# A hybrid layer's expert stage: rows spread over the dense blocks, half of the late query products moved into the second stage

## The reference, cut to what matters

```python
q = einsum('td,de->te', xb, w_q).reshape(T, 8, 2, 128)        # 8 heads, 2 halves
s = einsum('thpd,hpkd->thpk', q, keys)                         # 128 keys per half
s_top, i_top = top_k(s, 16)                                    # per half
best, sel = top_k(all 16 x 16 sums of the two halves, 16)
gate = softmax(best)
act = gelu(einsum('td,thkd->thk', xb, u_tab[eidx]))            # dot with the expert's row u
out = einsum('thk,thkd->td', gate * act, v_tab[eidx])          # weighted sum of the rows v
```

## Time and profile before

| what | value |
|---|---|
| median of 3 runs | 2141.62 us (2140.74 to 2150.80) |
| profiled execution, its own time | 2143.07 us |
| its span in the profile | 2141.0 us |
| TensorE matmul busy | 1934.9 us, 90% of the span |
| VectorE busy | 1358.9 us, 63% |
| ScalarE busy | 616.4 us, 29% |
| GpSimd busy | 675.5 us, 32% |
| DMA | 629.25 MB, mean 294 GB/s |
| granted TensorE clock, mean | 0.972 of full speed |
| dense stage (144 blocks) | about 844 to 1531 us |
| second stage (384 rows) | about 1535 us to the end |

### The profile page before, as it was taken

The page is one execution under the profiler, slowest core; times in us unless marked ns, Lnnn a source line. Parts: engine busy times, 40 slices in busy tenths (PEclk is TensorE's granted clock), DMA queues, the critical chain, the costliest instruction groups (busy, mean ns, idle before and its releaser), DMA issues.

```text
span 2141.0 us, 29757 instructions
## 1 busy us (share of the span) xinstructions
PE 1934.9 (90%) x10912; PEld 1564.2 (73%) x10912; DVE 1358.9 (63%) x2860; ACT 616.4 (29%) x1217; POOL 675.5 (32%) x556
## 2 busy tenths in 40 slices
PE   5998889988996988999999999998899998999886
PEld 4997889978966988998999999998544433434332
DVE  3219263353345535488988888988377777776663
ACT  4223312252224324444445444445300000000000
POOL 0003012100000000232333233232277776776663
PEclk9999899988998999999999999999999999999999
DMA  3557158637614573899999999999499999999997
GB/s 117 197 198 220 31 180 260 216 86 257 237 41 178 177 261 119 318 366 349 403 388 361 388 394 357 376 364 376 184 412 403 404 407 412 397 398 415 405 414 290
DMA packets 244650, 629.25 MB, mean 294 GB/s; under 512 B 19714, under 2 KB 137541, under 8 KB 226712
## 3 DMA queue, kind: packets, MB, share of 16 engines
q0 software_dynamic: 74880, 377.52, 44.5%
q1 hardware_dynamic: 169632, 249.92, 34.4%
HBM read 584.36 MB, written 110.21 MB: 324 GB/s over the span
## 4 chain that ended last, share of the span: by engine, by line
DMA 19%; PE 15%; DVE 14%; issue 7%; ACT 2%; POOL 2%; SPq 1%; DVEq 1%; another core or an unknown queue 0%; ACTq 0%; POOLq 0%
DMA ex_w_raw<-in_peer_ut 10%; DMA ex_uv_row<-value_rows,ex_eidx 9%; PE ps L2137 9%; DVE ex_fin L2388 4%; DVE ex_w_lo L1935 3%; POOL ex_uv_row L2066 2%; PE ps L589 2%; PE ps L590 2%; PE ps L591 2%; DVE ex_uv_row L2376 2%; ACT ex_w_hi L2199 1%; DVE ex_q_s L2401 1%; DVE ex_top_i L2335 0%; SPq L1989 0%; DVEq L162 0%
## 5 line engine op out<-in xcount | busy, mean ns | idle before, releaser
L2137 PE MATMUL ps<-ex_uv_row,ex_q_s 128*128 128x512 f32 (+1 forms) x1208 | 542.4, 599 | 61.3 <-DVE ex_q_s L2401 47.3
L2137 PEld LDWEIGHTS ps<-ex_uv_row,ex_q_s 128*128 128x128 f32 (+1 forms) x1208 | 217.1, 187 | 366.3 <-issue 347.6
L2066 POOL DMA_INDIRECT ex_uv_row<-value_rows,ex_eidx x384 | 405.2, 1055 | 214.6 <-issue 102.2
L589 PE MATMUL ps<-x_hi,ex_w_lo 128*128 128x384 f32 (+2 forms) x1296 | 427.6, 330 | 27.8 <-DVE ex_w_lo L1935 22.6
L590 PE MATMUL ps<-x_lo,ex_w_hi 128*128 128x384 f32 (+2 forms) x1296 | 423.6, 327 | 0.0
L591 PE MATMUL ps<-x_hi,ex_w_hi 128*128 128x384 f32 (+2 forms) x1296 | 423.5, 327 | 0.0
L2050 POOL DMA_INDIRECT ex_uv_row<-in_peer_uv,ex_eidx x128 | 190.6, 1489 | 410.2 <-DVE ex_fin L2388 404.7
L2388 DVE SCALAR_TENSOR_TENSOR ex_fin<-ex_uv_row,ret_tables,ex_fin 128x1024 f32<-128x1024 f32 x218 | 278.7, 1279 | 0.3
L589 PEld LDWEIGHTS ps<-x_hi,ex_w_lo 128*128 128x128 f32 x1296 | 244.6, 189 | 40.7 <-DVE ex_w_lo L1935 30.7
L591 PEld LDWEIGHTS ps<-x_hi,ex_w_hi 128*128 128x128 f32 x1296 | 245.0, 189 | 0.0
L590 PEld LDWEIGHTS ps<-x_lo,ex_w_hi 128*128 128x128 f32 x1296 | 244.8, 189 | 0.0
(11 more groups left out here) (415 smaller groups left out, 3418.5 us busy)
## 6 DMA issues: line engine op xcount, KB each, us to landing
value_rows<-in_peer_uv SPq DMA_DIRECT2D x64, 1024.0 KB
ex_w_raw<-in_peer_ut SPq DMA_DIRECT2D x128, 512.0 KB
value_rows<-ex_z_rows SPq DMA_DIRECT2D x128, 128.0 KB
first_raw<-in_w_in SPq DMA_DIRECT2D x8, 1024.0 KB, 7.9
ex_w_raw<-in_peer_wq SPq DMA_DIRECT2D x16, 512.0 KB
value_rows<-ex_z_rows SPq DMA_DIRECT2D x128, 64.0 KB
dp_w_raw<-in_w_in SPq DMA_DIRECT2D x14, 512.0 KB
ex_uv_row<-value_rows,ex_eidx POOLq DMA_INDIRECT x384
```

The costliest lines, as they stand in the source:

```text
L589: pe.matmul(out, left(llo, c), right(rhi, c), start=(c == 0), stop=False)
L2066: pool.indirect_dma_start(value_slot(p)[0], None, k.value_rows, bass.IndirectOffsetOnAxis(ap=eidx[:, u, n % TOPK:n % TOPK + 1], axis=0), e ...
L2137: ins = pe.matmul(k.pv[j % 2][0:r, c, :], spread[:, on_tensor[p] % SPREADS, 0:r], v[:, c * 512:(c + 1) * 512], start=first, stop=last)
```

## The change

It has five parts. (1) The last four heads' query blocks ("first", 8 of them) compute in the dense stage only the 136 columns of tile 0 and the sample tile. The 384 columns of tiles 1 to 3 ("rest", 8 blocks) come in the second stage, one in front of rows 8, 17, ..., 71 of it, with their 512 KB of weights loaded, rounded and lowered again. (2) The columns of the tokens are laid out as tile 0, sample, tiles 1 to 3, so that the first four heads' query blocks too are now two groups, of 136 and 384 columns, in place of 260 and 260. (3) Rows begin at block 6, none stands at a block whose number is a multiple of 16, and so 130 rows stand beside the dense blocks; the last 6, all of the sample tile, come behind them. (4) VectorE makes a block's lower half ahead of that block's dot. (5) 9 more rows of the second stage go to VectorE, and `norm_final` is loaded into the buffer `x_rep`, once all 136 dots are made. Three of the eight rest blocks' weights are still loaded beside the dense blocks, and two of them lowered there; SyncE loads the other five behind the results of the first two tiles.

```diff
-ROWS_FROM = 8
+ROWS_FROM = 6
+FULL = 4
+QUERY_ROWS = [8 + 9 * n for n in range(2 * (PH - FULL))]
...
-    for u in range(PH - 1):
-        out += [("q", 2 * (u + 1) + j // 3) if j in (0, 3) else ("z", next(z)) for j in range(TOPK)]
-    return out + [("z", n) for n in z]
+    for u in range(1, PH):
+        kind = "q" if u < FULL else "first"
+        out += [(kind, 2 * u + j // 3) if j in (0, 3) else ("z", next(z)) for j in range(TOPK)]
+    return out + [("z", n) for n in z], [("rest", n) for n in range(2 * FULL, HP)]
...
+    row_at = dict(zip((i for i in range(ROWS_FROM, B) if i % TOPK), range(PAIRS)))
+    beside = len(row_at)
+    query_at = {PAIRS + m: B + n for n, m in enumerate(QUERY_ROWS)}
...
-    by_vector = {*range(HK), *(rests - late), *range(SLOTS - VECTOR_LAST, SLOTS)}
+    more = {PAIRS + m for m in range(12, QUERY_ROWS[-1] + 9) if m % TOPK in (5, 13)}
+    by_vector = {*range(HK), *(rests - late), *more, *range(SLOTS - VECTOR_LAST, SLOTS)}
...
-        x_rep, gain = sb("x_rep", [P, D])[:, :], w_raw[1][:, :, :].rearrange("p c n -> p (c n)")
+        x_rep, gain = [sb("x_rep", [P, D])[:, :]] * 2
...
-        tile = lambda t: slice(t * P, t * P + ROWS[t])
+        at_column = lambda t: t * P + (NS if 0 < t < TILES else 0) if t < TILES else P
+        tile = lambda t: slice(at_column(t), at_column(t) + ROWS[t])
...
-                    if i == len(blocks) - 1:
-                        lowered(sp, len(blocks) - 2)
-                        sp.dma_start(gain, a["norm_final"].unsqueeze(0).to_broadcast([P, D])).then_inc(gain_loaded, 16)
                 store(blocks[-1][1])
-                for j in range(NT):
+                sp.wait_ge(dotted, PAIRS)
+                sp.dma_start(gain, a["norm_final"].unsqueeze(0).to_broadcast([P, D])).then_inc(gain_loaded, 16)
+                result(0)
+                result(1)
+                for i in range(B + DEEP, len(all_blocks)):
+                    load(i)
+                for j in range(2, NT):
                     result(j)
...
-                def queries(i, n):
+                def queries(i, kind, n):
                     lowered(pe, i)
-                    for h in range(2):
-                        wait(pe, q_done, 2 * n + h - 1)
-                        mm3(pe, k.pb[4 + h][:, 0:HALF], DC, lambda x, c: x[:, c, :], w_hi[i % DEEP], w_lo[i % DEEP],
-                            lambda x, c: x[:, c, h * HALF:(h + 1) * HALF], x_hi, x_lo).then_inc(q_mm, 1)
+                    if kind != "rest":
+                        wait(pe, q_done, n)
+                        mm3(pe, k.pb[4][:, 0:P + NS], DC, lambda x, c: x[:, c, :], w_hi[i % DEEP], w_lo[i % DEEP],
+                            lambda x, c: x[:, c, 0:P + NS], x_hi, x_lo).then_inc(q_mm, 1)
+                    if kind != "first":
+                        wait(pe, rest_done, n)
+                        mm3(pe, k.pb[5][:, 0:BT], DC, lambda x, c: x[:, c, :], w_hi[i % DEEP], w_lo[i % DEEP],
+                            lambda x, c: x[:, c, P + NS:T], x_hi, x_lo).then_inc(rest_mm, 1)
...
                 for p in range(PAIRS, SLOTS):
                     u, i = divmod(order[p], TOPK)
+                    if p in query_at:
+                        queries(query_at[p], *all_blocks[query_at[p]])
                     if p not in by_vector:
                         add_row(p)
...
+                    if query_at.get(p + 6, 0) >= B + 2:
+                        upper(query_at[p + 6])
+                    if p - 2 in query_at:
+                        take(*all_blocks[query_at[p - 2]])
...
-                for i in range(len(blocks)):
-                    p = i - ROWS_FROM
-                    if 0 <= p < PAIRS:
+                for i in range(B):
+                    p = row_at.get(i, -1)
+                    if i + 2 >= 5:
+                        lower(dve, i + 2)
+                    if p >= 0:
                         dot(p)
-                    if 5 <= i + 2 < len(blocks) and by_dve(i + 2):
-                        lower(dve, i + 2)
                     if 0 < p <= HK:
                         add_vector(p - 1)
...
-                for p in range(len(blocks) - ROWS_FROM, PAIRS):
+                for p in range(beside, PAIRS):
                     dot(p)
...
                 for p in range(PAIRS, SLOTS):
                     u, i = divmod(order[p], TOPK)
+                    if query_at.get(p + 4, 0) >= B + 2:
+                        lower(dve, query_at[p + 4])
                     picked(p)
```

More of the change, by code:

```diff
@@ L1999, in _ @@
                 for i, (kind, n) in enumerate(blocks):
[L2000 to L2001 removed]
+                    load(i + DEEP)
                     if i and blocks[i - 1][0] == "z":
@@ L2173, in _ @@
                 for i, (kind, n) in enumerate(blocks):
-                    if kind == "q":
-                        queries(i, n)
+                    if kind == "z":
+                        activities(i, n)
                     else:
-                        activities(i, n)
+                        queries(i, kind, n)
                     if i in scores_at:
                         scores(scores_at[i])
-                    if HK <= i - ROWS_FROM - 1 < PAIRS:
-                        add_row(i - ROWS_FROM - 1)
-                for p in range(len(blocks) - ROWS_FROM - 1, PAIRS):
+                    if row_at.get(i, 0) > HK:
+                        add_row(row_at[i] - 1)
+                for p in range(max(HK, beside - 1), PAIRS):
                     add_row(p)
@@ L2283, in _ @@
                     elif i:
-                        take(blocks[i - 1][1], 0)
-                        take(blocks[i - 1][1], 1)
-                    if i and i + 2 < len(blocks):
+                        take(*blocks[i - 1])
+                    if i:
                         upper(i + 2)
-                    if 0 <= i - ROWS_FROM < PAIRS:
-                        row(i - ROWS_FROM)
+                    if i in row_at:
+                        row(row_at[i])
                     if i in weight_at:
@@ L2480, in _ @@
                         normalise(normalise_at[i])
-                for p in range(len(blocks) - ROWS_FROM, PAIRS):
+                for p in range(beside, PAIRS):
                     dot(p)
+                    if p <= HK:
+                        add_vector(p - 1)
+                    if p == HK:
+                        add(0)
                 scale(0)
```

43 lines of the change are left out of this document (23 added, 20 removed).

## The result

| | before | after |
|---|---|---|
| median of 4 runs (lowest to highest) | 2141.18 us (2125.25 to 2150.80) | 2212.48 us (2204.76 to 2227.20) |
| profiled execution, its span | 2143.07, 2141.0 us | 2204.76, 2202.7 us |

What follows compares the result with a forecast made beforehand. The prediction took TensorE to lead in the dense stage, DMA and VectorE close, and DMA behind row 80. From 2143.07 us, -24 and +23.2 gave 2142.3, forecast as 2141 us, no measurable change; range 2120 to 2162.

Steps and rivals of the forecast that it cites:

- Lower half ahead of the dot: VectorE's dense-stage order: loads come a dot (1.22 us) earlier behind retrieval pieces, at most 4.9 us per period; nothing more counted.
- the weight loads decide: Rival, chance 0.26: weight loads landing near 13 us keep the four dense periods near 73 us; total about 2155 us.
- dense stage: Sum of the terms up to the last dense block: -24 us, with ends -6 and -40.
- passage: From the last dense block to the first value row: late `norm_final` delays `scale(0)`; +9.5 us, ends 4 and 17.
- first 80 rows: Start of the second stage: eight rest blocks add 33.8 us to TensorE, nine moved rows take 16.1 off; +17.7 us.
- behind row 80: Rest of the second stage: DMA bounds again, with ten rows ahead instead of seven or eight; -4 us, ends 0 and -10.
- second stage: Sum of everything behind the dense stage, passage included: +23.2 us, ends +12 and +32.
- 136 columns at 0.112 us: Query blocks' small matmuls: assumed to start every 0.112 us, as for 128 columns, making a first block 2.7 us.
- TensorE's 71.1 become 65.0: Blocks 50 to 114: TensorE's need per 16 blocks falls thus, period 74.25 to 69.5 us, gaining 19 us in all.
- TensorE leads: Dense stage before: TensorE's need per 16 blocks, 71.1 us, is the largest, ahead of DMA's 68.7 and VectorE's 64.6.
- The rest blocks are free: Rival, chance 0.11: ten slots and TensorE's idle time absorb them; second stage costs 10 instead of 23.2; total 2128 us.
- the dense stage reaches the DMA floor: Rival, chance 0.18: the four periods fall to 67 us, the last stretch gives all 10.9, passage 5 cheaper; total 2123 us.

Runs made afterwards that it cites:

- e2: The kernel before with only VectorE's lower half moved ahead of the dot: 2207.62 us, ratio 1.0307 to the kernel before.
- e5: The changed kernel, lower half still first, with ScalarE making at each block the coefficient of the row before: 2134.37 us, ratio 0.9987 to the kernel before.
- e3: The kernel before with only the rows' new places (from block 6, none at multiples of 16, six sample rows behind the dense stage): 2128.83 us, ratio 0.994.
- e8: The kernel before with the rows' new places, lower half first and coefficient one row behind, query blocks as before: 2126.09 us, ratio 0.9934.
- e6: The changed kernel with the dot first again and `norm_final` loaded eight dots earlier, into `x_first`: 2134.56 us, ratio 0.9988 to the kernel before.
- e4: The changed kernel with the dot first again, without the move of query blocks and its nine rows: 2141.26 us, ratio 0.9981 to the kernel before.
- e11: e8 with `norm_final` issued behind the last block's store instead of ahead of it: 2125.36 us, ratio 0.9914 to the kernel before.

## Why the prediction was wrong

**The step that failed** is "Lower half ahead of the dot", with "In the cycle lower, dot, sum the order is the old one" and "If the load isn't late, it is worth 0". It looked at VectorE alone and asked only how early the lower half comes. It did not follow the dot, whose result ScalarE waits for, one instruction ahead of its next rounding. The measured price is 66 us (e2) to 73 us (after against e1). The warning stood in the trace of before: ScalarE waited 126.6 us, 76 times, for dots in 940 to 1500, nearly as much as for loads, and the prediction did not take that line in. No rival named the loop; "the weight loads decide" was on the right side by sign and wrong by mechanism, since that wait fell.

**The rest of the sum** can be held against the two kernels in which the ring is open: e1, the change without that step, 2139 us, and e5, the change with the coefficient one row behind, 2134 us, where 2141 was forecast. In their profiled runs, against the one of before:

| term (us) | forecast | e1 | e5 |
|---|---|---|---|
| blocks 0 to 17 | +2 | +6.1 | +9.0 |
| blocks 18 to 50 | +3 | -4.2 | -1.2 |
| blocks 50 to 114 | -19 | -12.3 | -20.1 |
| blocks 114 to 130 | -2 | -1.5 | -4.0 |
| blocks 130 to E | -8 | -10.3 | -8.9 |
| dense stage | -24 | -22.2 | -25.2 |
| passage | +9.5 | +5.1 | +10.6 |
| first 80 rows | +17.7 | +13.0 | +11.3 |
| behind row 80 | -4 | 0 | 0 |
| second stage | +23.2 | +18.2 | +21.8 |

The first term is what is left of the dense stage. The totals are right to 5 us. Part of that is luck: in both, the first blocks cost more than forecast and the later ones less, and the rows behind row 80 gave nothing back while the first 80 cost less.

- *136 columns at 0.112 us*: right. The changed kernel's timeline has 22 of them from one start to the next between these two rows, (1098.41 - 1095.96)/22 = 0.111:

```profile
1095.96 0.27 PE L592 MATMUL ps<-x_lo,ex_w_hi 128*128 128x136 f32 x1
...
1098.41 0.28 PE L593 MATMUL ps<-x_hi,ex_w_hi 128*128 128x136 f32 x1
```

- *The dense gain* was put down to "TensorE's 71.1 become 65.0". e3 has 12.9 us of it with TensorE's need unchanged, by the rows' places alone, down to the 71.1 of that need. So "TensorE leads" holds for e3; in the kernel before, TensorE took 13 us more than its need. What the move adds depends on the order: nothing in e1 (285.3 against e3's 284.7), 9.1 us in e5 (277.5 against e8's 286.6). The 69.5 us per period of the forecast, 3.4 above a DMA need "at the second stage's 407 GB/s", were met in e5 (69.4) and missed in e1 (71.3). Neither moved 407 GB/s there, but 388 and 378.
- *The passage*: the forecast let `norm_final` land 6.6 us after its issue and end last. In e5 it did so, 1525.59 - 1518.21 = 7.4 us after it, and the term came true. In e1 it was there after at most 1522.68 - 1518.60 = 4.1 us (and at least 3.5, since the wait outlasted the root, which ended at 1522.11), and the +5.1 have another reason: the first value gather starts 9.4 us behind E instead of 3.5, after the last block's store, where the prediction let it follow at once. It also did not count ScalarE's root, which in e3 and e6 is what `scale(0)` waits for. The rule of the Trainium skill ("DMA: Bandwidth & Descriptors", Queues, rings and completion order) had given an estimate of 2.6 us; both measured values are longer.
- *The first 80 rows*: the mechanism was right, TensorE's work plus the rest blocks. In 1577 to 1718 of the changed kernel TensorE is busy for 136.7 of 141 us. Before, 120.4 us lay between the first value row and row 80, after it 133.5: +13.1 against 17.7. Nothing was caught up behind row 80.
- *"The rest blocks are free"* and *"the dense stage reaches the DMA floor"*: the first did not come, the second stage paid for them. The second did not come either: no run got below 69.4 us per period, where the rival said 67.
- *"The weight loads decide"*: its own formula gives (13 + 1.06 + 1.22)/3 = 5.1 us per block with a landing of 13, 81 per period, and not the 73 that it says.

**Still open**: why e5 moves the same bytes faster than e1 in blocks 50 to 114 (388 and 378 GB/s), and both slower than the second stage (405 to 407); what holds the kernel before 13 us above TensorE's need there; why e4 also loses 5 us in blocks 114 to 130, where no query block stands; and what holds the last store besides the 512 KB that e11 moved from ahead of it, since the gathers in flight were not varied by themselves.
